# Three blocks on one Trainium2 core: decays of the state-space chunks from differences of prefix sums, and x weighed on GpSimd

## The chip, the core and the metric

The program runs on one core of one Trainium2 chip. The metric is the time of one execution on the device in microseconds (us), the median of the runs. Engines: TensorE (PE, its weight loads PEld), VectorE (DVE), ScalarE (ACT), GpSimd (POOL) and SyncE (SP), which here only asks for transfers.

## What is computed

Three blocks follow one another on x of 1024 tokens by 1024 features in fp32: stick-breaking attention with SwiGLU, a convolution and retention block, and a block with an S5 branch and a state-space branch (SSD) side by side. The change lies in the SSD branch alone. It has 16 heads of width 64, 4 groups, a state of 128:

```python
xd = (xs * dt[..., None])                       # x weighed by its step width
a = dt * A;  a_cs = jnp.cumsum(a, axis=-1)      # A < 0, one value per head
L_intra = jnp.exp(segsum(a))                    # exp(cs[l] - cs[s]) for s <= l, else 0
y_diag = einsum(einsum(Ch, Bh) * L_intra, xd)   # within a chunk
decay_states = jnp.exp(a_cs[..., -1:] - a_cs)   # x weighed by its decay to the chunk's end
states = einsum(Bh, decay_states, xd)           # carried on from chunk to chunk
y_off = einsum(Ch, prev_states, jnp.exp(a_cs))
y = gated_group_rmsnorm(y_diag + y_off + D * xs, z, norm_w)
```

## The kernel before

Everything is feature-major: 8 tiles of 128 features by 1024 tokens. Nearly all of TensorE's time goes into weight products in three parts (x high and low by w high and low, L650, L653, L654); GpSimd splits each weight panel into high and low parts (L609, L611, and L597 for panels that carry gains), SP loads the panels. Each engine has its own program, written out by hand in order, and waits on counters.

**The SSD stage** (ssd_out, about 3110 to 3248 us) takes 8 chunks of 128 tokens. All inputs are already in DRAM (spills). For chunk c, SP loads f (x, B and C of the chunk, 1 MB, double-buffered, L572) and zf (the gate z, L576). In the order of TensorE's queue:

- turn_x (L1221) transposes x; ScalarE copies it to xt (L1922); VectorE makes xd = xt * dt (L2769) and xe = xd * decay (L2781)
- turn_y (L1290) of the chunk before; scores (L1233) C by B; VectorE masks them into sm (L2786)
- decays (L1245): four products of the 0/1 matrix "after" with mt. mt holds, for each of 16 heads, the matrix "upto" times the step decays da (16 small ScalarE activations, L1781). The product is the sum of the decays between two tokens; ScalarE takes its Exp into lt (L1932); VectorE multiplies lt by sm (L2794)
- turn_b (L1228), direct (L1256, D * x), inter (L1272, C by the state), sums (L1299, the norm's sums of the chunk before, from ScalarE's Square L1945), intra (L1262, lt by xd), new (L1282, B by xe)

VectorE adds up y (L2802, L2808) and the state (L2813, L2818), makes the low part of the result before (low, L2842), the gate product gz (L2830) and the scaling (L2836). ScalarE's order for a step is: xt, Exp, bt (L1939), Square of the chunk before, half of mt for the chunk after next, the norm's Ln and Exp (L1950, L1953), the other half of mt, xh (L1957). Behind the Exp of chunk 0 ScalarE also asks for h back from DRAM (4 MB, L1964).

**Ahead of it**, the last tiles of xBC and of z run, and between their halves TensorE does the S5 outputs (s5_outputs, L775), whose results ScalarE's queue stores by 8 transfers each (y_store, L1824). At xBC tile 15 TensorE forms the prefix sums of da for all chunks (dec_sum, L1199) into bank 3. In the first z_last tile ScalarE makes mt of chunk 0. dec (L1914) is the Exp of the prefix sums, the tail sums and the totals; TensorE's first turn_x waits for it. On SP, the loads of f stand behind the last weight panels, and eight stores of the last S5 outputs (L581) behind zf of chunk 1.

Of the kernel before, what the change touches and what calls it, by code (L numbers as in the profile page):

```python
# [13 lines left out]
P = 128  # L14
# [249 lines left out]
def build(nc, ins, out, last=None):  # L264
# [5 lines left out]
    with ctx:  # L270
# [141 lines left out]
        with ExitStack() as st:  # L412
# [6 lines left out]
            mt = sb("mt", [P, SSD_HEADS, P], F32, st)  # L419
# [23 lines left out]
        y_spill = dram("y_spill", [D, S5_TAU, S5_BLOCKS])  # L443
        h_spill = dram("h_spill", [P, KT, T])
# [3 lines left out]
        seg_banks = [5, 0, 1, 5]  # L448
# [68 lines left out]
        def _(sp):  # L517
# [29 lines left out]
            else:  # L547
# [40 lines left out]
        def _(pool):  # L588
# [24 lines left out]

            def turn(name, i, before):
# [33 lines left out]
        def _(pe):  # L648
# [515 lines left out]
            if "s5_u" in run:  # L1164
# [37 lines left out]

                def within_xbc(e):
# [10 lines left out]
                for m in range(2):  # L1214
                    tile_x(units("z_last") + 2 * m, panels("z_last") + m, between=lambda: s5_outputs(6 + m))

            def ssd_turn_x(c):

                pe.wait_ge(S(f"f_in{c % 2}"), (c // 2 + 1) * 16)
                for q in range(8):  # L1220
# [16 lines left out]
            def ssd_decays(c):  # L1237

                pe.wait_ge(S("mt_ready"), c + 1)
                for q in range(4):  # L1240
                    if q == 1:
                        pe.wait_ge(S("xt_ready"), c + 1)
                    if q == 3:
                        pe.wait_ge(S("lt_ready"), 4 * c + 1)
                    nc.tensor.matmul(banks[seg_banks[q]][:, :], M["after"],  # L1245
                                     mt[:, 4 * q:4 * q + 4, :].rearrange("p h t -> p (h t)"),
                                     start=True, stop=True).then_inc(S("seg_done"), 1)

# [18 lines left out]
            def ssd_inter(c):  # L1267
                pe.wait_ge(S("state_ready"), c + 1)
                pe.wait_ge(S("sm_ready"), c + 1)
                pe.wait_ge(S("lt_ready"), 4 * c + 4)  # L1270
# [43 lines left out]
            if "ssd_out" in run:  # L1314
# [5 lines left out]
                ssd_decays(0)  # L1320
                ssd_turn_b(0)
                ssd_direct(0)
                for c in range(CHUNKS):
# [34 lines left out]
        def _(act):  # L1358
# [416 lines left out]
            def ssd_steps(c, part):  # L1775

                act.wait_ge(S("da_ready"), 1)
                if c:
                    act.wait_ge(S("seg_done"), 4 * c)
                for hd in range(8 * part, 8 * part + 8):  # L1780
                    mm = A(mt[:, hd, :], M["upto"], ACT.Copy, scale=da[:, c, hd:hd + 1])  # L1781
                if part:
                    mm.then_inc(S("mt_ready"), 1)

            if "s5_u" in run:
# [127 lines left out]
                act.wait_ge(S("dec_sum"), 1)  # L1913
# [11 lines left out]
            def ssd_exp(c):  # L1925
# [4 lines left out]
                for q in range(4):  # L1930
# [29 lines left out]
            if "ssd_out" in run:  # L1960
# [5 lines left out]
                for part in range(2):  # L1966
                    ssd_steps(1, part)
                for c in range(CHUNKS):
# [74 lines left out]
        def _(dve):  # L2043
# [711 lines left out]
            def heads(t, q):  # L2755
                return t[:, q * 512:(q + 1) * 512].rearrange("p (h d) -> p h d", d=SSD_P)

            def per_head(t, q):
                return t[:, 8 * q:8 * q + 8].unsqueeze(2).broadcast_to([P, 8, SSD_P])

            def ssd_weigh_x(c):

                dve.wait_ge(S("xt_ready"), c + 1)
                if c:
                    dve.wait_ge(S("intra_done"), c)
                else:
                    dve.wait_ge(S("spilled0"), 16 * 20)
                for q in range(2):
                    mm = V.tensor_tensor(heads(xd, q), heads(xt, q), per_head(dt[:, c, :], q), ALU.mult)  # L2769
                mm.then_inc(S("xd_ready"), 1)  # L2770

            def ssd_decay_x(c):

                dve.wait_ge(S("xd_ready"), c + 1)
                dve.wait_ge(S("dec_ready"), 1)
# [285 lines left out]
```

## Time and profile before

| what | us |
|---|---|
| median of 3 runs (lowest, highest) | 3666.65 (3662.11, 3667.56) |
| the profiled execution's own time | 3663.11 |
| its span | 3661.3 |
| PE busy | 3538.3 (97%) |
| DVE, POOL, ACT busy | 2080.5, 1093.3, 935.3 |

The span is what the profiler saw from the first to the last instruction; the time also holds what lies around it. Matmuls are pipelined: a matmul's duration is longer than the step to the next one, so the chain of waits, which counts from step to step, tells what a group of them costs.

### The profile page before, as it was taken

How to read it: one execution, taken by the hardware profiler on the slowest of the kernel's cores; microseconds unless marked ns; L12 is line 12 of the kernel's file. 1: busy time of each engine (PE TensorE's matmuls, PEld its weight loads, DVE VectorE, ACT ScalarE, POOL GpSimd, SP SyncE). 2: the span in 40 equal slices, each digit the busy share in tenths (PEclk: the TensorE clock that was granted, in tenths of full speed). 3: DMA queues.
4: the chain of work that ended last, by engine and by line, in shares of the span. 5: the costliest groups of instructions: out<-in, count | busy, mean ns of one | idle time of the engine just before them, and what ended most of it. 6: DMA issues, size and time to landing. Idle time of an engine off the chain costs nothing. (4 is left out here: it accounts for less than half of the span.)

```text
span 3661.3 us, 46083 instructions
## 1 busy us (share of the span) xinstructions
PE 3538.3 (97%) x18166; PEld 2876.8 (79%) x18166; DVE 2080.5 (57%) x2838; ACT 935.3 (26%) x1662; POOL 1093.3 (30%) x1069
## 2 busy tenths in 40 slices
PE   7999999999999999999999999799999999999998
PEld 5777776688888888788888888588878878787776
DVE  6464557524233236699945555644535697753564
ACT  4444445300000004311111100411221123652132
POOL 2221121233333333233332233033332234024332
PEclk9999999999999999999999999999999999999999
DMA  2010010212212111122221121221293224432211
GB/s 100 24 30 30 24 35 13 75 58 62 70 57 74 57 57 58 35 98 86 86 81 70 41 81 65 91 87 41 87 181 86 82 78 131 145 103 75 73 54 64
DMA packets 139240, 260.19 MB, mean 71 GB/s; under 512 B 45632, under 2 KB 87616, under 8 KB 136000
## 3 DMA queue, kind: packets, MB, share of 16 engines
q1 hardware_dynamic: 73360, 156.78, 14.7%
q10 hardware_dynamic: 65712, 101.10, 8.1%
q8 instruction: 114, 1.87, 0.2%
q14 instruction: 54, 0.44, 0.0%
HBM read 209.35 MB, written 46.14 MB: 70 GB/s over the span
## 5 line engine op out<-in xcount | busy, mean ns | idle before, releaser
L650 PE MATMUL bank<-xh,wh 128*128 128x512 f32 x3024 | 1192.8, 394 | 30.1 <-DVE xl L2107 12.1
L653 PE MATMUL bank<-xl,wh 128*128 128x512 f32 x3024 | 1183.1, 391 | 0.0
L654 PE MATMUL bank<-xh,wl 128*128 128x512 f32 x3024 | 1181.9, 391 | 0.0
L609 POOL CAST wh<-raw 128x512 fp32r<-128x512 f32 x528 | 345.7, 655 | 2364.4 <-PE bank L654 2202.5
L611 POOL TENSOR_TENSOR wl<-raw,wh 128x512 fp32r<-128x512 f32 x528 | 733.9, 1390 | 42.3
L650 PEld LDWEIGHTS bank<-xh,wh 128*128 128x128 f32 x3024 | 569.4, 188 | 168.0 <-issue 18.7
L654 PEld LDWEIGHTS bank<-xh,wl 128*128 128x128 f32 x3024 | 569.5, 188 | 122.3 <-issue 0.7
L653 PEld LDWEIGHTS bank<-xl,wh 128*128 128x128 f32 x3024 | 570.0, 188 | 118.0 <-issue 1.3
L2407 DVE SCALAR_TENSOR_TENSOR bank<-apad,cols,bank 128x512 f32<-128x512 f32 x406 | 267.9, 751 | 0.0
L2145 DVE TENSOR_TENSOR h<-bank,h 128x512 f32<-128x512 f32 x240 | 165.6, 691 | 145.5 <-PE bank L654 144.8
L2276 DVE TENSOR_TENSOR gt<-sa,bank 128x512 f32<-128x512 f32 x44 | 30.3, 688 | 347.8 <-PE bank L654 347.8
L2242 DVE TENSOR_TENSOR_SCAN fb<-fb,own_key 128x256 f32<-128x256 f32 (+7 forms) x128 | 174.3, 1403 | 68.4 <-ACT ab L1469 68.3
L650 PE MATMUL bank<-wh,xh 128*128 128x256 f32 x512 | 148.0, 289 | 0.4 <-POOL wl L611 0.4
L653 PE MATMUL bank<-wl,xh 128*128 128x256 f32 x512 | 144.8, 283 | 0.0
L654 PE MATMUL bank<-wh,xl 128*128 128x256 f32 x512 | 144.7, 283 | 0.0
L650 PE MATMUL bank<-gh,wh 128*128 128x512 f32 x352 | 138.2, 393 | 0.0
L654 PE MATMUL bank<-gh,wl 128*128 128x512 f32 x352 | 137.1, 390 | 0.0
L653 PE MATMUL bank<-gl,wh 128*128 128x512 f32 x352 | 136.9, 389 | 0.0
L2148 DVE SCALAR_TENSOR_TENSOR h<-bank,mod,h 128x512 f32<-128x512 f32 x128 | 95.3, 750 | 69.6 <-PE bank L654 69.0
L1521 ACT ACTIVATE sa<-bank 128x512 f32<-128x512 f32 x44 | 26.3, 599 | 390.1 <-DVE msum L2312 258.9
L2709 DVE SCALAR_TENSOR_TENSOR spill<-xc,cols,spill 128x1024 f32<-128x1024 f32 x48 | 69.0, 1438 | 96.5 <-ACT spill L1844 95.3
L1468 ACT ACTIVATE fb<-bank 128x512 f32<-128x512 f32 (+2 forms) x192 | 95.9, 500 | 87.7 <-PE bank L905 87.4
(339 smaller groups left out, 4876.9 us busy)
## 6 DMA issues: line engine op xcount, KB each, us to landing
raw<-in_wstream SPq DMA_DIRECT2D x264, 512.0 KB, 3.5
spills<-spill ACTq DMA_DIRECT2D x38, 512.0 KB, 2.9
rawm<-in_mod_w ACTq DMA_DIRECT2D x12, 1024.0 KB, 4.9
gate_spill<-gates ACTq DMA_DIRECT2D x16, 512.0 KB, 2.6
tabs<-in_rope ACTq DMA_DIRECT2D x4, 2048.0 KB, 8.9
f<-spills SPq DMA_DIRECT2D x8, 1024.0 KB, 5.6
h<-in_x ACTq DMA_DIRECT2D x4, 1024.0 KB, 11.8
tabs<-gate_spill ACTq DMA_DIRECT2D x4, 1024.0 KB, 7.4
```

Source lines behind the costliest of these rows:

```text
L609: nc.gpsimd.tensor_copy(wh[:, slot, k], raw[:, slot, k]).then_inc(S("panel_high"), 1)
L611: nc.gpsimd.tensor_tensor(wl[:, slot, k], raw[:, slot, k], wh[:, slot, k].bitcast(F32), ALU.subtract).then_inc(S("panel_split"), 1)
L650: mm = nc.tensor.matmul(o, lh, rh, start=start, stop=False, skip_group_check=shared)
L653: nc.tensor.matmul(o, lh, rl, start=False, stop=False, skip_group_check=shared)
L654: return nc.tensor.matmul(o, ll, rh, start=False, stop=stop, skip_group_check=shared)
L1468: A(fb[:, g % 2, a, s], banks[2 + n % 3][:, :w], ACT.Sigmoid, scale=-1.0)
L2145: V.tensor_tensor(h[:, n, t], banks[th][:, :], h[:, n, t], ALU.add).then_inc(S(f"bank_free{th}"), 1)
L2148: V.scalar_tensor_tensor(h[:, n, t], banks[th][:, :], gates(n), h[:, n, t], ALU.mult, ALU.add).then_inc(S(f"bank_free{th}"), 1)
L2242: V.tensor_tensor_scan(f_, f_, own_key[:, T - w:T][:, ::-1], 0.0, ALU.mult, ALU.max).then_inc(S("scanned"), 1)
L2276: V.tensor_tensor(gt[:, th, :], sa[:, th, :], banks[u.b % 2][:, :], ALU.mult).then_inc(S(f"bank_free{u.b % 2}"), 1)
L2407: V.scalar_tensor_tensor(o, a_in, w, o, ALU.mult, ALU.add).then_inc(S("conv_step"), 1)
L2709: V.scalar_tensor_tensor(o, a_in, w, o, ALU.mult, ALU.add).then_inc(S("x_step" if k < SSD_TAPS - 1 else "xo_ready"), 1)
```

## The change

The sum of decays between two tokens is the difference of two prefix sums. TensorE's decays products and ScalarE's mt go. Instead the prefix sums from dec_sum are copied with their sign turned into dtmp (one column per chunk and head), transposed by TensorE (cs_turn), copied again and stored to DRAM (cs_rows, 64 KB). SP loads for each chunk the rows of its 16 heads, the same 8 KB to all 128 partitions (csb, 1 MB). ScalarE forms |csb + dtmp| for each head (16 Abs), then four Exp with scale -1. The mask is applied in four parts, and intra waits for each. xd and xe are made by GpSimd.

```diff
-            mt = sb("mt", [P, SSD_HEADS, P], F32, st)
+            csb = sb("csb", [P, SSD_HEADS, P], F32, st)
...
+        cs_rows = dram("cs_rows", [P, P])
-        seg_banks = [5, 0, 1, 5]
+        cs_turned = msum[:, 0:P]
...
@@ SyncE, before the loads of f and zf of chunk c
                 for c in range(CHUNKS):
+                    if c:
+                        sp.wait_ge(S("lt_spans"), 4 * c)
+                    else:
+                        sp.wait_ge(S("cs_stored"), 16)
+                        sp.wait_ge(S("pc_ready"), KT)
+                    sp.dma_start(csb[:, :, :].rearrange("p h t -> p (h t)"),
+                                 cs_rows.rearrange("(c h) t -> c (h t)", c=CHUNKS)[c:c + 1].broadcast_to(
+                                     [P, SSD_HEADS * P])).then_inc(S("csb_in"), 16)
...
@@ GpSimd, behind the split of the first two ssd_out panels; both functions as VectorE had them, on pool
+                if name == "ssd_out" and i is None:
+                    for c in range(CHUNKS):
+                        ssd_weigh_x(c)
+                        ssd_decay_x(c)
...
@@ TensorE
+                def cs_turn():
+                    pe.wait_ge(S("cs_kept"), 1)
+                    nc.tensor.transpose(banks[2][:, 0:P], dtmp[:, :, :].rearrange("p c h -> p (c h)"), M["ident"]
+                                        ).then_inc(S("dec_sum"), 1)
...
-                    tile_x(units("z_last") + 2 * m, panels("z_last") + m, between=lambda: s5_outputs(6 + m))
+                    def within_z():
+                        if m == 0:
+                            cs_turn()
+                        s5_outputs(6 + m)
+
+                    tile_x(units("z_last") + 2 * m, panels("z_last") + m, between=within_z)
...
             def ssd_turn_x(c):
+                if c:
+                    pe.wait_ge(S("xt_ready"), c)
...
-            def ssd_decays(c):
...
             def ssd_intra(c):
-                pe.wait_ge(S("w_masked"), c + 1)
+                pe.wait_ge(S("xd_ready"), c + 1)
                 for hd in range(SSD_HEADS):
+                    if hd % 4 == 0:
+                        pe.wait_ge(S("w_masked"), 4 * c + hd // 4 + 1)
...
@@ ScalarE
-            def ssd_steps(c, part):
...
+                act.wait_ge(S("dec_sum"), 1)
+                A(dtmp[:, :, :].rearrange("p c h -> p (c h)"), banks[3][:, 0:P], ACT.Copy, scale=-1.0
+                  ).then_inc(S("cs_kept"), 1)
                 for m in range(2):
                     unit = units("z_last") + 2 * m
...
                     if m == 0:
-                        act.wait_ge(S("pc_ready"), KT)
-                        for part in range(2):
-                            ssd_steps(0, part)
                         y_store(6)
+                        act.wait_ge(S("dec_sum"), 2)
+                        A(cs_turned, banks[2][:, 0:P], ACT.Copy, scale=-1.0).then_inc(S("cs_kept"), 1)
+                        act.wait_ge(S("cs_kept"), 2)
+                        act.dma_start(cs_rows[:, :], cs_turned).then_inc(S("cs_stored"), 16)
...
@@ ScalarE, ssd_exp(c)
-                for q in range(4):
-                    act.wait_ge(S("seg_done"), 4 * c + q + 1)
-                    A(lt[:, 4 * q:4 * q + 4, :], banks[seg_banks[q]][:, :].rearrange("p (h t) -> p h t", t=P),
-                      ACT.Exp).then_inc(S("lt_ready"), 1)
+                act.wait_ge(S("csb_in"), 16 * c + 16)
+                for hd in range(SSD_HEADS):
+                    mm = A(lt[:, hd, :], csb[:, hd, :], ACT.Abs, bias=dtmp[:, c, hd:hd + 1])
+                    if hd % 4 == 3:
+                        mm.then_inc(S("lt_spans"), 1)
+                for g in range(SSD_GROUPS):
+                    act.wait_ge(S("lt_spans"), 4 * c + g + 1)
+                    A(lt[:, 4 * g:4 * g + 4, :], lt[:, 4 * g:4 * g + 4, :], ACT.Exp, scale=-1.0
+                      ).then_inc(S("lt_ready"), 1)
...
@@ VectorE, ssd_weights(c); its calls of ssd_weigh_x and ssd_decay_x go
-                V.tensor_tensor(l4, l4, sm[:, :, :].unsqueeze(2).broadcast_to([P, SSD_GROUPS, 4, P]), ALU.mult
-                                ).then_inc(S("w_masked"), 1)
+                for g in range(SSD_GROUPS):
+                    dve.wait_ge(S("lt_ready"), 4 * c + g + 1)
+                    l4 = lt[:, 4 * g:4 * g + 4, :]
+                    V.tensor_tensor(l4, l4, sm[:, g, :].unsqueeze(1).broadcast_to([P, 4, P]), ALU.mult
+                                    ).then_inc(S("w_masked"), 1)
```

What this does to the order of instructions, at three places.

ScalarE ahead of the stage: the copy of the prefix sums (dtmp) between the eight stores of y_store(5) and the first half of z's first tile (xd). Before:

```order
L1824 DMA y_spill<-u 16x8x128 [waits s5_added]
L1824 DMA y_spill<-u 16x8x128 x7
L1899 ACTIVATE xd<-bank 128x512 [waits unit_done]
L1830 ACTIVATE spill<-spill 128x1024 [waits xo_ready]
L1832 DMA spills<-spill 128x1024 [waits xs_ready]
L1899 ACTIVATE xd<-bank 128x512 [waits unit_done]
L1906 DMA spills<-xd 128x1024 [waits spilled0,bank_free1,bank_free0]
L1781 ACTIVATE mt<-mats,da 128x128 [waits da_ready,pc_ready]
L1781 ACTIVATE mt<-mats,da 128x128 x7
```

Now, with msum the transposed sums:

```order
L1856 DMA y_spill<-u 16x8x128 [waits s5_added]
L1856 DMA y_spill<-u 16x8x128 x7
L1928 ACTIVATE dtmp<-bank 128x128 [waits dec_sum]
L1934 ACTIVATE xd<-bank 128x512 [waits unit_done]
L1862 ACTIVATE spill<-spill 128x1024 [waits xo_ready]
L1864 DMA spills<-spill 128x1024 [waits xs_ready]
L1934 ACTIVATE xd<-bank 128x512 [waits unit_done]
L1941 DMA spills<-xd 128x1024 [waits spilled0,bank_free1,bank_free0]
L1856 DMA y_spill<-u 16x8x128 [waits s5_added]
L1856 DMA y_spill<-u 16x8x128 x7
L1945 ACTIVATE msum<-bank 128x128 [waits dec_sum]
L1947 DMA cs_rows<-msum 128x128 [waits cs_kept]
```

The copy into dtmp is new in front of the xd eviction, and the 16 mt activations are replaced by one copy and a store behind y_store(6).

ScalarE in one step of the loop (from taking x of chunk c+1 to xh of chunk c). Before:

```order
L1922 ACTIVATE xt<-bank 128x512 [waits xd_ready,x_turned]
L1922 ACTIVATE xt<-bank 128x512
L1932 ACTIVATE lt<-bank 128x512 [waits seg_done,intra_done]
L1932 ACTIVATE lt<-bank 128x512 [waits seg_done] x3
L1939 ACTIVATE bt<-bank 128x512 [waits new_done,b_turned]
L1945 ACTIVATE sq<-gz 128x1024 [waits ssd_sum,gz_ready]
L1781 ACTIVATE mt<-mats,da 128x128 [waits seg_done,da_ready]
L1781 ACTIVATE mt<-mats,da 128x128 x7
L1950 ACTIVATE bank<-bank,eps 128x512 [waits ssd_sum]
L1953 ACTIVATE bank<-bank 128x512 [waits rs_log]
L1781 ACTIVATE mt<-mats,da 128x128 [waits seg_done,da_ready]
L1781 ACTIVATE mt<-mats,da 128x128 x7
```

Now:

```order
L1957 ACTIVATE xt<-bank 128x512 [waits xd_ready,x_turned]
L1957 ACTIVATE xt<-bank 128x512
L1967 ACTIVATE lt<-csb,dtmp 128x128 [waits csb_in,intra_done]
L1967 ACTIVATE lt<-csb,dtmp 128x128 x15
L1972 ACTIVATE lt<-lt 128x512 [waits lt_spans] x4
L1979 ACTIVATE bt<-bank 128x512 [waits new_done,b_turned]
L1985 ACTIVATE sq<-gz 128x1024 [waits ssd_sum,gz_ready]
L1990 ACTIVATE bank<-bank,eps 128x512 [waits ssd_sum]
L1993 ACTIVATE bank<-bank 128x512 [waits rs_log]
L1997 ACTIVATE xh<-gz 128x8x128 [waits gn_ready]
```

The 16 small activations, before in two halves behind the Square (sq), are now ahead of Exp, bt and the Square.

SP at the first two chunks, before (u is the S5 output) and now:

```order
L572 DMA f<-spills 128x16x128 [waits spilled1,spilled0]
L576 DMA zf<-spills 128x8x128 [waits spilled1,spilled0]
L572 DMA f<-spills 128x16x128
L576 DMA zf<-spills 128x8x128
L581 DMA y_spill<-u 16x8x128 [waits s5_added]
```

```order
L580 DMA csb<-cs_rows 128x2048 [waits pc_ready,cs_stored]
L588 DMA f<-spills 128x16x128 [waits spilled1,spilled0]
L592 DMA zf<-spills 128x8x128 [waits spilled1,spilled0]
L580 DMA csb<-cs_rows 128x2048 [waits lt_spans]
L588 DMA f<-spills 128x16x128
L592 DMA zf<-spills 128x8x128
L597 DMA y_spill<-u 16x8x128 [waits s5_added]
```

A load of csb is new in front of each load of f, and the second one waits for lt_spans, the Abs of chunk 0.

## Rows read from the trace of the kernel before

**Rows 1.** The page, part 1: busy time, share of the span, instructions

```profile
PE 3538.3 (97%) x18166; PEld 2876.8 (79%) x18166; DVE 2080.5 (57%) x2838; ACT 935.3 (26%) x1662; POOL 1093.3 (30%) x1069
```

**Rows 2.** Chain of waits, one chunk (3179 to 3197) and one start: start us, us, line

```profile
3128.04 0.87 PE bank L1221 x8
...
3179.17 0.87 PE bank L1221 x8
...
3181.81 3.44 PE bank L1245 x8
...
3185.68 1.79 PE bank L1256 x16
3187.47 1.73 PE bank L1272 x8
3189.20 1.72 PE bank L1299 x4
3190.91 3.52 PE bank L1262 x32
...
3196.22 0.87 PE bank L1221 x8
```

**Rows 3.** Timeline of ScalarE: start us, us, line, operation, count [idle before]

```profile
3118.32 4.78 ACT L1781 ACTIVATE mt<-mats,da 128x128 f32<-128x128 f32 x16
...
3180.08 1.08 ACT L1922 ACTIVATE xt<-bank 128x512 f32<-128x512 f32 x2 [1.60 <-PE bank L1221]
...
3186.26 1.06 ACT L1945 ACTIVATE sq<-gz 128x1024 f32<-128x1024 f32 x1
```

**Rows 4.** Timeline of VectorE, the same chunk

```profile
3181.40 1.22 DVE L2842 TENSOR_TENSOR xl<-gz,xh 128x1024 fp32r<-128x1024 f32 x1
3182.54 1.29 DVE L2769 TENSOR_TENSOR xd<-xt,dt 128x512 f32<-128x512 f32 x2
3183.74 1.28 DVE L2830 TENSOR_TENSOR gz<-zf,bank 128x512 f32<-128x512 f32 x2
```

**Rows 5.** Timeline of TensorE, entry to the stage

```profile
3086.29 2.15 PE L775 MATMUL bank<-h,pb 64*128 64x127 f32 x32
...
3110.43 1.94 PE L1221 MATMUL bank<-mats,f 128*128 128x128 f32 x8 [3.14 <-ACT dec L1914]
```

**Rows 6.** Timeline of ScalarE, the same entry

```profile
3084.26 5.80 ACTq L1824 DMA_DIRECT2D y_spill<-u  x8
...
3094.82 0.36 ACTq L1906 DMA_DIRECT2D spills<-xd  x1
```

**Rows 7.** TensorE, timeline, then a stretch: us, PE busy, PEclk, DMA share, GB/s

```profile
2337.23 0.47 PE L650 MATMUL bank<-rh,wh 128*128 128x512 f32 x1 [1.97 <-DVE h L2148]
...
2338.70:2342.10 3.40, 2.82 (x8) 0.50 0.45 154
```

**Rows 8.** DMA, 3060 to 3262: issuer, count, KB, us to landing; SP's timeline

```profile
f<-spills SPq DMA_DIRECT2D x8, 1024.0 KB, 5.6
...
h<-h_spill ACTq DMA_DIRECT2D x1, 4096.0 KB, 14.4
...
y_spill<-u ACTq DMA_DIRECT2D x30, 64.0 KB, 2.9
...
y_spill<-u SPq DMA_DIRECT2D x8, 64.0 KB, 11.8
...
3094.67 0.39 SPq L572 DMA_DIRECT2D f<-spills  x1
```

**Rows 9.** DMA queues, 3117 to 3132: packets, MB, share of 16 engines

```profile
q10 hardware_dynamic: 144, 4.19, 71.2%
q1 hardware_dynamic: 2117, 1.01, 23.0%
```

**Rows 10.** Lines L597 (GpSimd) and L2709 (VectorE): ns min/median/max

```profile
L597 POOL TENSOR_TENSOR raw<-raw,cols x8: 1890/1898/2882, 3083.2 to 3308.0; 128x1024 f32<-128x1024 f32 x8
...
L2709 DVE SCALAR_TENSOR_TENSOR spill<-xc,cols,spill x48: 1270/1285/2806, 2665.6 to 3087.2; 128x1024 f32<-128x1024 f32 x48
```

More of the change, by code:

```diff
@@ L446, in build, with heads, per_head @@
         block = ctx.enter_context(nc.Block())
-        seg_banks = [5, 0, 1, 5]
+        cs_turned = msum[:, 0:P]
+        def heads(t, q):
+            return t[:, q * 512:(q + 1) * 512].rearrange("p (h d) -> p h d", d=SSD_P)
+        def per_head(t, q):
+            return t[:, 8 * q:8 * q + 8].unsqueeze(2).broadcast_to([P, 8, SSD_P])
         def settled(eng):
@@ L612, in split, with ssd_weigh_x, ssd_decay_x @@
                                             ALU.subtract).then_inc(S("panel_split"), 1)
+            def ssd_weigh_x(c):
+                pool.wait_ge(S("xt_ready"), c + 1)
+                if c:
+                    pool.wait_ge(S("intra_done"), c)
+                else:
+                    pool.wait_ge(S("spilled0"), 16 * 20)
+                for q in range(2):
+                    mm = nc.gpsimd.tensor_tensor(heads(xd, q), heads(xt, q), per_head(dt[:, c, :], q), ALU.mult)
+                mm.then_inc(S("xd_ready"), 1)
+            def ssd_decay_x(c):
+                pool.wait_ge(S("xd_ready"), c + 1)
+                pool.wait_ge(S("dec_ready"), 1)
+                if c:
+                    pool.wait_ge(S("new_done"), c)
+                else:
+                    pool.wait_ge(S("spilled1"), 16 * 20)
+                for q in range(2):
+                    mm = nc.gpsimd.tensor_tensor(heads(xe, q), heads(xd, q), per_head(dec[:, 1, c, :], q), ALU.mult)
+                mm.then_inc(S("xe_ready"), 1)
             def turn(name, i, before):
@@ L1214, in _ @@
                 for m in range(2):
-                    tile_x(units("z_last") + 2 * m, panels("z_last") + m, between=lambda: s5_outputs(6 + m))
+                    def within_z():
[3 more added lines that the diff above has]
+                    tile_x(units("z_last") + 2 * m, panels("z_last") + m, between=within_z)
             def ssd_turn_x(c):
                 pe.wait_ge(S(f"f_in{c % 2}"), (c // 2 + 1) * 16)
+                if c:
+                    pe.wait_ge(S("xt_ready"), c)
                 for q in range(8):
@@ L1235, in ssd_scores @@
                 mm.then_inc(S("bc_done"), 1)
-            def ssd_decays(c):
-                pe.wait_ge(S("mt_ready"), c + 1)
-                for q in range(4):
[L1241 to L1247, printed above, removed]
             def ssd_direct(c):
@@ L1773, in spill_tiles @@
                         act.dma_start(spills[n * 2 + (first + m)], spill[:, m, :]).then_inc(S(f"spilled{m}"), 16)
-            def ssd_steps(c, part):
[L1777 to L1783, printed above, removed]
             if "s5_u" in run:
@@ L1929, in ssd_exp @@
                     act.wait_ge(S("intra_done"), c)
-                for q in range(4):
-                    act.wait_ge(S("seg_done"), 4 * c + q + 1)
-                    A(lt[:, 4 * q:4 * q + 4, :], banks[seg_banks[q]][:, :].rearrange("p (h t) -> p h t", t=P),
-                      ACT.Exp).then_inc(S("lt_ready"), 1)
+                act.wait_ge(S("csb_in"), 16 * c + 16)
[7 more added lines that the diff above has]
+                      ).then_inc(S("lt_ready"), 1)
             def ssd_take_b(c):
@@ L1965, in _ @@
                 ssd_take_b(0)
-                for part in range(2):
-                    ssd_steps(1, part)
                 for c in range(CHUNKS):
@@ L2753, in _ @@
                 s5_add(7)
[L2755 to L2775, printed above, removed]
-                if c:
-                    dve.wait_ge(S("new_done"), c)
-                else:
-                    dve.wait_ge(S("spilled1"), 16 * 20)
-                for q in range(2):
-                    mm = V.tensor_tensor(heads(xe, q), heads(xd, q), per_head(dec[:, 1, c, :], q), ALU.mult)
-                mm.then_inc(S("xe_ready"), 1)
             def ssd_mask(c):
@@ L2844, in _ @@
             if "ssd_out" in run:
-                ssd_weigh_x(0)
-                ssd_decay_x(0)
                 ssd_mask(0)
@@ L2865, in _ @@
                         ssd_weights(c + 1)
-                        ssd_decay_x(c + 1)
                     ssd_scale(c)
```

12 lines of the change are left out of this document (removed).

## The prediction

> **What bounds the kernel now.** I read the page's busy shares first, then the chain of waits in the stage that changes, then what ScalarE and VectorE do there, then the entry to the stage and its transfers. TensorE is busy for 97% of the span [rows 1], so what matters is TensorE's queue. The chain shows what it does in one chunk of the state-space stage [rows 2]: from one turn of x (L1221) to the next it is 3196.22 - 3179.17 = 17.05 us, all of it TensorE, without a gap. Of this the decay sums (L1245) take 3.44 us. ScalarE and VectorE are hidden under it. So taking L1245 out promises 8 x 3.44 = 27.5 us, and the question is what stands right behind TensorE, and what the replacement costs at the entry. A measurement of this kernel can tell about 0.2%, 7.3 us, from no change.
>
> **The steady chunk.** TensorE's own work falls to 17.05 - 3.44 = 13.61 us. Before, the 16 small activations of a chunk (mt) ran two chunks ahead, in ScalarE's idle time. Their successors, 16 Abs of the same 128x128 form, stand in ssd_exp: behind take_x of the same chunk, and ahead of take_b and of the previous chunk's Square. That closes a loop, because TensorE's order is inter(c+1), sums(c), intra(c+1), and sums(c) waits for that Square. With its pieces, counted from the end of intra(c): new (L1282, from 3190.91 + 3.52 = 3194.43 to 3196.22, 1.78 in the chain) and turn_x 0.87 [rows 2] make 2.65. Taking x is two evictions, 0.98 before the next may start (1.08 for both, the second's end overlapping) [rows 3]. For the 16 Abs no row exists. The nearest is the mt group: 16 in 4.78, one every 0.29, so 4.69 of occupancy [rows 3]; the bounds are 3.2 (if a read of plain data with a bias took 0.2 each) and 6.3 (each at its full 0.39, if nothing overlapped). I take 4.69, the same shape. Then 4 Exp at the eviction's 0.49, 1.96; one eviction for b, 0.49; Square 1.06 [rows 3]. Then sums 1.72 and intra 3.52 [rows 2]. The sum is 2.65 + 0.98 + 4.69 + 1.96 + 0.49 + 1.06 + 1.72 + 3.52 = 17.07, and with some 0.2 for handing over between engines 17.3 us. So **the loop through ScalarE is as long as the TensorE work that it replaces**: 7 chunks x (17.3 - 17.05) = **+1.8 us**. With the bounds of Abs it is 15.8 to 18.9 a chunk, -9 to +13.
>
> What lies beside it: xd and xe move to GpSimd, 4 operations of 128x512 a chunk. The nearest GpSimd row multiplies by a broadcast column, 128x1024 in 1.90 [rows 10], so about 1.0 each and 4 us; up to 5.8 if it is disturbed as in that group's longest, 2.88. They begin when x is taken (3.6) and are done by 7.6 to 9.4, while intra wants xd at 13.6 and new wants xe at 17. They cost nothing; cover gone, the bill starts only above 6 us more. VectorE loses 2.6 us of work in a chunk. Splitting the mask into four lets it follow each Exp. VectorE still has to give the gate. In the chunk before, intra (L1262) ended at 3194.43 - 17.05 = 3177.4 and gz at 3183.74 + 1.28 = 3185.0, 7.6 later, with 1.2 of xd ahead of it that goes away [rows 2, 4]: gz at 6.4, then direct (1.79) and inter (1.73) to 9.9 [rows 2], against the Square's end at 11.8. That is 1.9 us of slack. GpSimd's work falls on this very piece. In the one place where a three-operation VectorE group meets a GpSimd multiply, one VectorE operation of 1.28 became 2.81 and GpSimd's 1.90 became 2.88 [rows 10]: both slowed down, together about by the shorter one's length. One such meeting (low with xd) is about 1 us and fits in the slack. The Trainium skill (SBUF — State Buffer, its table of terms) says that the pair of ports is locked for a whole instruction and the loser blocks fully; by it low could wait for both xd operations, and the sum would be up to 3 us longer over 7 chunks.
>
> **Entry, the new wait.** cs_turn stands on TensorE between the two halves of the first z_last tile, where it waits for ScalarE's copy of the prefix sums (cs_kept). In ScalarE's queue this copy is behind the 8 store issues of y_store(5), which last until 3084.26 + 5.80 = 3090.06 [rows 6]. TensorE is there at 3086.29 [rows 5]. The copy takes 0.39 like mt, so TensorE stands from 3086.3 to about 3090.6: 4.3 us, and queued behind it are s5_outputs(6) and the half tile; z's evictions, y_store(6), the last outputs and dec wait for those. After a wait of 3.14 us before 3110.43, eight transposes took 1.94 [rows 5] where the chain has 0.87 for the same eight [rows 2]; behind a shorter wait elsewhere the granted clock was 0.50, 1.2 GHz, through a stretch of 3.4 us [rows 7]. Such a stretch does half of its work; the same after this wait costs some 1.7. With the transpose **+6.1 us**.
>
> **Entry, the transfers.** Before, f of chunk 0 was asked for at 3094.67 and lay ready long before turn_x(0) at 3110.43 [rows 5, 8]. Now SP first waits for cs_stored. z's store goes out at 3094.82 + 6.1 = 3100.9 [rows 6]; y_store(6) takes 5.8 as y_store(5) did; the copy and its issue 0.8; a 64 KB store 2.9 to land [rows 8]. So csb(0) is asked for at about 3110.4. f takes 5.6 alone; csb is as large (1024 KB) and in the same queue ahead of it. h, four times as large, lands in 14.4, so 1 MB more is some (14.4 - 5.6) / 3 = 2.9, say 3.0 [rows 8]: f(0) lands 5.6 + 3.0 = 8.6 after, at 3119.0, a little later with z's spill between. turn_x(0) starts at 3119.7 where it could have at 3110.43 + 6.1 = 3116.5: **+3.2 us**. Bounds: 0 (csb lands for nothing) and 6 (128 reads of one 8 KB row at half the rate).
>
> **Chunk 0.** Before, 3128.04 - 3110.43 = 17.61 from turn_x(0) to turn_x(1) [rows 2, 5]. Now, with the first transposes at the low clock as before: 1.94 + 0.98 + 4.69 + 1.96, the last quarter of the mask 0.7 (low is 1.22 for twice the columns), the last quarter of intra 0.9, new 1.78 = 12.95, since nothing of a chunk before stands in between. **-4.7 us.** VectorE's dd is ready earlier, too, without xd and xe.
>
> **f of chunk 1.** This is the largest term. f(1) was issued at once behind f(0); now it is behind csb(1), and that waits for the Abs of chunk 0 (lt_spans), 1.94 + 0.98 + 4.69 = 7.6 after turn_x(0) begins. At the same moment ScalarE, past its Exp, asks for h (4096 KB, 14.4 to land) [rows 8]. What such a neighbour does can be seen: eight 64 KB stores of SP that lie beside h took 11.8 to land, ScalarE's own of that size 2.9 [rows 8]; and while h moved, its queue passed 144 packets with 4.19 MB and SP's queue 1.01 MB in 2117 small ones, most of them before h began or after it ended [rows 9]. So packets take turns, not bytes. csb(1) has 8 KB packets against h's 32 KB ones, and f(1), of 512 B packets behind csb, gets little until both are done. h landed 14.4 after its issue with 0.5 MB of stores beside it; csb is 0.5 MB more, 1.6; then f's 3.0. f(1) lands 7.6 + 19.0 = 26.6 after turn_x(0), while TensorE is ready at 12.95. **+13.7 us**, and 0.9 for a cold clock after it. Bounds: csb and f alone need 8.6, so f at 16.2, +3.3; all of csb behind all of h, +15. I take the value near the upper bound, since the stores beside h behaved so. In later chunks f is asked for at 8.8 of the loop and wanted at 17.3 + 1.8 = 19.1, over 10 us later; 8.6 fits.
>
> **Clock in between.** The new loop leaves TensorE idle for 17.3 - 13.6 = 3.7 us a chunk in two pieces, 1.6 before direct (from turn_b's end at 4.8) and 1.9 before sums. After a wait of 1.97 at 2337 the clock was at 0.50 for the next stretch [rows 7]. Part of this lies under slack; **+1.5 us** in all, between 0 and 12.
>
> **The sum:** 6.1 + 3.2 - 4.7 + 13.7 + 0.9 + 1.8 + 1.5 = +22.5, on the profiled execution's 3663.11, which is 3.5 under the median of the runs shown. On the median 3666.65 it is 3689.
>
> **Rivals.**
> (1) f(1) is less late, since the queues share by bytes, or csb slips in ahead of h. Then the 13.7 falls to between 3 and 7: 3678 to 3682. Against it are the 11.8 us stores.
> (2) The clock falls in every chunk. Each fall is a stretch of 3.4 us at half speed, 1.7 lost: 7 x 1.7 = 12, less the 1.5 counted: 3699.5. For it: the 1.97 row; against it: most of a gap here is shorter. The Trainium skill (TensorE: Matmul & The Clock Gate, HAM oscillation) describes exactly this, a loop with a wait in each round that starts cold each time; the trace shows single cases of it only.
> (3) GpSimd blocks VectorE for all its 4 us: gz at 10.4, direct and inter to 13.9, past the Square by 2.1, 7 x 2.1 = 15: 3704. For it: both operands of low lie in SBUF like those of the disturbed row; against it: gate and mask read a bank, and VectorE's operations of that kind showed no such stretching.
> (4) The other side: faster. If the ScalarE steps between turn_x and sums(c) come to 3 us less than my 9.2 (Abs at 0.2 each and Exp from SBUF cheaper), the loop is 14.3, nearly TensorE's 13.6, and 7 chunks give -19; with the entry (+9.3 - 4.7) and f(1) hidden by half (+6) 3658. It decides below a loop of 14.5 us. Against it is the row of 16 in 4.78.
> (5) No change: the entry wait is small and f(1) nearly in time: -4.7 + 1.8 and some 4, 3668.
>
> **How the numbers follow.** My forecast 0.47 (its own range 3683 to 3695), rival 1 0.19, rival 2 0.12, rival 3 0.10, rival 4 0.05, rival 5 0.07. Slower by over 0.2% (above 3674): 0.47 + 0.19 + 0.12 + 0.10 = 0.88; within: 0.07; faster: 0.05. The range 3674 to 3702 leaves out rivals 4 and 5 and half of 3.
>
> **What would show it.** Right: a TensorE wait of about 4 us for a transpose of dtmp at 3086; turn_x(0) waiting for f, not dec; a wait of over 10 us for f before turn_x(1), with csb and f landing late beside h; a period of 17.3 with Square waiting for nothing and sums waiting for Square; no wait for xd or xe. Wrong: a period near 13.6 to 15 us, f(1) landing within 9 us of csb's issue, or direct waiting for gz longer than sums for Square.

## The result, and the profile after

| what | before | after |
|---|---|---|
| median of 5 runs (lowest, highest) | 3665.72 (3662.11, 3667.56) | **3685.29** (3683.16, 3688.55) |
| span of the profiled execution | 3661.3 | 3683.5 |
| PE, DVE, POOL, ACT busy | 3538.3, 2080.5, 1093.3, 935.3 | 3520.8, 2068.5, 1133.1, 933.6 |

The kernel is slower by 0.55%: the ratio is 1.0055, with a 95% interval of 1.0044 to 1.0066, so 19.6 us at the medians. TensorE works 17.5 us less than in [rows 1] and the time grows, so in the profiled executions, whose spans differ by 22.2, it stands idle for some 40 us more. The waits of TensorE say where.

TensorE's waits in the changed kernel from 3060 to 3300 us (line, what it waited for: us in all, times, longest):

```profile
PE bank L1299 <- DVE gz L2836: 15.6, 6, 2.6
PE bank L1276 <- DMA f<-spills: 10.6, 1, 10.6
PE bank L1343 <- ACT sq L1985: 5.1, 5, 1.7
PE bank L1248 <- ACT dtmp L1928: 3.5, 1, 3.5
PE bank L1276 <- ACT dec L1949: 3.1, 1, 3.1
PE bank L1299 <- DVE dd L2854: 2.5, 1, 2.5
```

Here L1276 is turn_x, L1299 direct, L1343 sums, L1248 the transpose cs_turn. Only the wait for dec was there at this size before [rows 5].

TensorE's timeline at the entry, in chunks 0 and 1 (start us, us, line, operation, count, idle before it):

```profile
3093.40 0.34 PE L1248 MATMUL bank<-mats,dtmp 128*128 128x128 f32 x1 [3.50 <-ACT dtmp L1928]
3093.66 3.71 PE L818 MATMUL bank<-h,pb 64*128 64x127 f32 x32
...
3119.37 1.06 PE L1276 MATMUL bank<-mats,f 128*128 128x128 f32 x8 [3.14 <-ACT dec L1949]
...
3124.26 3.68 PE L1299 MATMUL bank<-dd,f 128*128 128x128 f32 x16 [2.50 <-DVE dd L2854]
...
3133.03 1.95 PE L1326 MATMUL bank<-xe,bt 128*128 128x256 f32 x8
3145.57 1.97 PE L1276 MATMUL bank<-mats,f 128*128 128x128 f32 x8 [10.60 <-DMA f<-spills]
```

**Entry.** cs_turn waits for the copy into dtmp, and the 32 small products behind it (L818) take 3.71 where they took 2.15 [rows 5]: a wait, then the low clock. turn_x of chunk 0 starts 8.9 us later than before [rows 5]. Not all of it is the change's: TensorE came to this place at 3089.9 where it had come at 3086.3 [rows 5], and the program up to there is the same on it. The 3.6 us are there at 2720 already: TensorE's waits for the low parts of weights from GpSimd add up to 12.6 there and to 9.0 in the kernel before. It is taken as scatter between executions: in the experiments, none of which changes TensorE's work up to there, it came between 3083.9 (e5) and 3093.2 (e8). The rest, 8.94 - 3.6 = 5.3, belongs to the change: the wait of 3.50, the transpose 0.26, and 3.71 - 2.15 = 1.56 for the low clock. turn_x of chunk 0 waits for dec, not for f.

**The second f.** DMA issues between 3126 and 3131 us (what, issuer, count, KB, us to landing):

```profile
h<-h_spill ACTq DMA_DIRECT2D x1, 4096.0 KB, 16.5
csb<-cs_rows SPq DMA_DIRECT2D x1, 1024.0 KB, 16.4
f<-spills SPq DMA_DIRECT2D x1, 1024.0 KB, 18.9
```

csb, h and f are asked for within half a microsecond; csb and h land together, and f, which stands behind csb, 2.9 us later. csb comes in 128 pieces of 8 KB and h in 128 of 32 KB, and the pieces of both run through the whole of this time side by side. Over all 8 chunks csb takes a median of 4.8, beside h 16.4. That is f's 10.6 us wait.

**The loop.** ScalarE and VectorE in one steady chunk, then GpSimd:

```profile
3182.70 1.09 ACT L1957 ACTIVATE xt<-bank 128x512 f32<-128x512 f32 x2 [2.55 <-PE bank L1276]
3183.68 4.78 ACT L1967 ACTIVATE lt<-csb,dtmp 128x128 f32<-128x128 f32 x16
3188.35 2.18 ACT L1972 ACTIVATE lt<-lt 128x512 f32<-128x512 f32 x4
3190.43 0.58 ACT L1979 ACTIVATE bt<-bank 128x512 f32<-128x512 f32 x1
3190.91 1.05 ACT L1985 ACTIVATE sq<-gz 128x1024 f32<-128x1024 f32 x1
```

```profile
3184.02 1.97 DVE L2848 TENSOR_TENSOR xl<-gz,xh 128x1024 fp32r<-128x1024 f32 x1
3186.12 1.29 DVE L2836 TENSOR_TENSOR gz<-zf,bank 128x512 f32<-128x512 f32 x2
```

```profile
3183.87 3.02 POOL L638 TENSOR_TENSOR xd<-xt,dt 128x512 f32<-128x512 f32 x2 [12.42 <-ACT xt L1957]
```

ScalarE goes from xt to Square without a gap, as foretold. low (L2848) takes 1.97 instead of 1.22 [rows 4], because xd on GpSimd lies beside it, and gz follows it. Of xd's two operations the first takes 1.04, as it does alone, and the second, beside low, 2.02. The chain shows the period (start us, us, line):

```profile
3164.23 0.89 PE bank L1276 x8
...
3181.79 0.89 PE bank L1276 x8
```

3181.79 - 3164.23 = 17.56, against 17.05 before [rows 2]. From turn_x of chunk 1 to turn_y of chunk 7 it is 3145.57 to 3270.71, 125.1 us against 119.3 before: in three places there the clock falls as well, as it does at the entry and in direct of chunk 0. Three of these five stretches (from:to us, length, busy time of the engines, PEclk, DMA share, GB/s):

```profile
3093.30:3096.60 3.30, 3.20 (x27) 3.08 (x29) 0.00 (x0) 1.48 (x3) 0.00 (x0) 0.54 0.44 143
3137.70:3151.20 13.50, 5.63 (x27) 5.63 (x28) 1.50 (x3) 3.63 (x12) 2.38 (x3) 0.51 0.76 222
3206.00:3209.20 3.20, 3.20 (x14) 2.89 (x13) 2.50 (x4) 3.20 (x7) 0.58 (x1) 0.54 0.71 220
```

The granted clock near 0.5 is the 1.2 GHz level. The second stretch begins inside the wait for f and holds on through the first products after it; the third follows the wait for gz.

### The profile page after: what moved, and what is told of

Same layout as the page of the kernel before. It is cut to its first block and busy times, and to the rows that moved or that the text cites. A ratio compares the mean times of both kernels' runs of the same rounds, so it can differ in the third digit from the quotient of the medians.

```text
span 3683.5 us, 45993 instructions
## 1 busy us (share of the span) xinstructions
PE 3520.8 (96%) x18103; PEld 2871.0 (78%) x18103; DVE 2068.5 (56%) x2830; ACT 933.6 (25%) x1664; POOL 1133.1 (31%) x1101
## 5 line engine op out<-in xcount | busy, mean ns | idle before, releaser
L693 PEld LDWEIGHTS bank<-xh,wh 128*128 128x128 f32 x3024 | 568.5, 188 | 172.7 <-issue 22.2
```

Source lines behind the costliest of these rows:

```text
L693: mm = nc.tensor.matmul(o, lh, rh, start=start, stop=False, skip_group_check=shared)
```

## The experiments

The theory has four parts: the copy's place in ScalarE's queue costs some 5 us, h beside csb and f some 10, the Square behind Abs and Exp the loop, and GpSimd's half little. The main rival was that low's slowing by GpSimd rules the loop. Each kernel was timed against the kernel before on the same chip; ratios are to that one, with 95% intervals. An interval reaches 4 to 6 us to either side, about what a single edit is worth, so for single edits the waits in the trace carry the verdict and the time supports it. A second measure leaves out what happens ahead of the stage: in the profiled execution, the time from where TensorE is ready for the transpose of dtmp (in the kernel before, for the S5 products behind it) to turn_y of chunk 7. It is 160.9 in the kernel before and 180.7 in the changed one (one execution of each).

### e1_copy_early: the copy into dtmp earlier in ScalarE's queue

```diff
 first_tap(e)
+if e == 15:
+    act.wait_ge(S("dec_sum"), 1)
+    A(dtmp..., banks[3][:, 0:P], ACT.Copy, scale=-1.0).then_inc(S("cs_kept"), 1)
...
-act.wait_ge(S("dec_sum"), 1)
-A(dtmp..., banks[3][:, 0:P], ACT.Copy, scale=-1.0).then_inc(S("cs_kept"), 1)
```

> The changed kernel with one edit: ScalarE copies the prefix sums into dtmp before Silu of xBC tile 14 and the eight stores of y_store(5), instead of behind them. If the 3.50 us that TensorE stood before the transpose of dtmp comes from those stores alone: no wait there (under 0.3), the S5 products behind it back from 3.71 to 2.15 us, so turn_x(0) about 5 us earlier and the time about 5 us shorter, 3680 against 3685. Rival (the wait is absorbed later by the load of f for chunk 0, which the transfers then delay): turn_x(0) waits for f instead of dec and the time moves by under 2 us.

3680.38, ratio 1.0045 (1.0028 to 1.0063). TensorE's timeline:

```profile
3085.68 0.27 PE L1248 MATMUL bank<-mats,dtmp 128*128 128x128 f32 x1
3085.88 2.15 PE L818 MATMUL bank<-h,pb 64*128 64x127 f32 x32
...
3110.03 1.94 PE L1276 MATMUL bank<-mats,f 128*128 128x128 f32 x8 [3.14 <-ACT dec L1950]
```

The wait is gone, the 32 products are back at 2.15, and turn_x of chunk 0 is where it was before. So the wait and its cold clock were the entry's 5.3 us. From the transpose to turn_y(7) it is 176.6, 4.0 less than in the change: turn_x(0) runs at the low clock again, 1.94 instead of 1.06.

### e2_h_late: h is fetched behind the last step of chunk 1

```diff
 ssd_take_x(0)
 ssd_exp(0)
-act.wait_ge(S("s5_carried"), KT)
-act.dma_start(h[:, :, :], h_spill[:, :, :])
 ssd_take_b(0)
 ...
     ssd_high(c)
+    if c == 1:
+        act.wait_ge(S("s5_carried"), KT)
+        act.dma_start(h[:, :, :], h_spill[:, :, :])
```

> The changed kernel with one edit: ScalarE asks for h (4 MB) behind chunk 1's last step instead of behind the Exp of chunk 0. If f(1) is late because csb(1) takes turns with h packet by packet: csb(1) lands in about 5 us instead of 16.4, f(1) in 7.5 instead of 18.9, TensorE's wait for f before turn_x(1) falls from 10.6 to under 1.5 us, and the time is 9 to 12 us shorter, unless h then delays the load of a later chunk by as much: h beside csb(2) or csb(3) would show the same wait of 8 to 11 us at that chunk. Rival (csb itself, 128 reads of the same 8 KB, is slow and h does not matter): the wait stays above 8 us and csb(1) stays above 12.

3677.68, ratio 1.0037 (1.0025 to 1.0048). Issues in the same place, without h:

```profile
csb<-cs_rows SPq DMA_DIRECT2D x1, 1024.0 KB, 4.7
f<-spills SPq DMA_DIRECT2D x1, 1024.0 KB, 7.5
```

TensorE waits for no f. From turn_x(0) to turn_x(1) it is 17.05 instead of 26.2, that is 9.1 less. The time falls by 7.6, where 9 to 12 was expected; to turn_y(7) the trace has 173.3, 7.3 less. Some of it is given back in the next chunk:

```profile
3144.46 3.42 PE L1343 MATMUL bank<-sq,mats 128*128 128x512 f32 x4 [3.15 <-ACT sq L1985]
```

With f early, TensorE is ahead of ScalarE, stands 3.15 for the Square and runs the sums at the low clock. Further on, h lies beside the transfers of a later chunk, where they have time: no wait.

### e10_f_first: SP asks for f ahead of csb

```diff
 for c in range(CHUNKS):
+    ...
+    sp.dma_start(f[:, c % 2], spills[3 * KT:3 * KT + 16, :, t]...)
     if c:
         sp.wait_ge(S("lt_spans"), 4 * c)
     ...
     sp.dma_start(csb..., cs_rows...)
-    ...
-    sp.dma_start(f[:, c % 2], spills[3 * KT:3 * KT + 16, :, t]...)
```

> The changed kernel with one edit on SP: in each chunk f is asked for ahead of csb. f(1) is then on its way before h. Theory (csb takes turns with h packet by packet, whatever stands behind it): TensorE's wait for f before turn_x(1) is gone, but csb(1), asked for at the same moment as before, still lands 15 to 16.5 us later, and now ScalarE's Abs of chunk 1 wait for it. The wait moves and shrinks, since xt and the rest of chunk 0 are done by then: about 6 us gained of the 10.6, 3679 to 3681 against 3685. Rival (f was late for its own small packets, csb does not matter): Abs of chunk 1 do not wait, 10 us or more gained, 3675 or less.

3682.80, ratio 1.0047 (1.0033 to 1.0062), only 2.5 less than the change where 4 to 6 was expected, and too little to tell from none by the time alone. f(1) lands in 6.2 and TensorE doesn't wait for it, but csb now takes up to 17.7. ScalarE's waits, then TensorE's timeline:

```profile
ACT lt L1967 <- DMA csb<-cs_rows: 6.6, 1, 6.6
```

```profile
3154.64 3.43 PE L1343 MATMUL bank<-sq,mats 128*128 128x512 f32 x4 [9.86 <-ACT sq L1985]
```

ScalarE waits 6.6 for csb in front of its Abs of chunk 1, and TensorE 9.86 for the Square behind them. The wait moved from one engine's operand to another's, and the sums behind it run at the low clock. From turn_x(0) to turn_x(2) it is 42.5 instead of 44.7. It is h beside the two, far more than their order, that costs.

### e3_square_first: Square ahead of the four Exp

```diff
     mm.then_inc(S("lt_spans"), 1)
+if c:
+    ssd_square(c - 1)
 for g in range(SSD_GROUPS):
```

> The changed kernel with one edit: Square of the chunk before stands between the Abs and the Exp of ssd_exp, instead of behind Exp and the eviction of b. Theory (the loop of 17.56 us runs through ScalarE up to Square and sums): Square ends 2.4 us earlier, sums follows inter without a wait, and the loop falls to what VectorE then allows: from sums through the norm's root, VectorE's eight operations up to gz (9.6), direct, inter and sums (5.2), 16.3 us; 6 loops give 7 to 8 us less, 3677 to 3679. Rival (the loop was bound by gz, late because of GpSimd): 17.5 us still, no change. Rival (TensorE's own 13.6 us is what is left): 14 us a loop, 20 us less.

3674.60, ratio 1.0035 (1.0025 to 1.0046). TensorE's timeline:

```profile
3193.63 1.04 PE L1276 MATMUL bank<-mats,f 128*128 128x128 f32 x8
...
3199.47 2.05 PE L1299 MATMUL bank<-dd,f 128*128 128x128 f32 x16 [2.59 <-DVE gz L2839]
...
3210.10 1.04 PE L1276 MATMUL bank<-mats,f 128*128 128x128 f32 x8
```

The period falls from 17.56 to 16.47 (16.3 was expected), and no wait for the Square is left. From turn_x(1) to turn_y(7) it is 117.4 instead of 125.0, the 7 to 8 us of the theory; the medians differ by more, 10.7. So the Square's place did set the loop. But it does not fall to TensorE's 13.6: a second loop stands right behind. The chain of this kernel gives its pieces, from sums to sums: sums 1.73, ScalarE's Ln and Exp of the norm 0.67 and 0.59, VectorE's scale 1.16, ys 2.60, state 2.54, low 1.90, gz 1.34, direct 2.05, inter 1.73, with the gaps 16.47 (3186.78 to 3203.25). It goes through VectorE.

### e4_weigh_vectore and e7_vectore_square_first: xd and xe back on VectorE

The same edit once in the changed kernel (e4) and once in e3 (e7):

```diff
 # GpSimd
-for c in range(CHUNKS):
-    ssd_weigh_x(c)
-    ssd_decay_x(c)
 # VectorE
     if c:
         ssd_low(c - 1)
+    if c + 1 < CHUNKS:
+        ssd_weigh_x(c + 1)
     ssd_gate(c)
     ...
         ssd_weights(c + 1)
+        ssd_decay_x(c + 1)
```

> The changed kernel with xd and xe back on VectorE, at their old places. Theory (ScalarE's loop is the bound, VectorE has slack): low falls from 1.97 to 1.2 us, xd takes 1.2 in its place, gz comes at the same moment or 0.3 us later, the loop stays at 17.6, and in chunk 0 the later dd vanishes in the wait for f(1): the time is the same within 2 us. Rival (GpSimd's work held up VectorE and so the loop): 1 us less a loop, 7 us less in all. Rival (the move to GpSimd is worth the 2.6 us a chunk that VectorE loses): 10 us or more longer.

> e3 (Square between Abs and Exp) with xd and xe on VectorE. In e3 VectorE's chain up to gz bounds the loop, at 16.46. If that is so, work put back on it now shows: xd 1.2 us more ahead of gz, low 0.75 less without GpSimd beside it, so 16.9 to 17.4 a loop, 3 to 6 us more than e3's 3674.6. Rival (xd and xe never matter): 16.46 still and the same time within 1.5 us.

e4: 3687.68, ratio 1.0062 (1.0045 to 1.0080), which can't be told from the change's 1.0055. The period stays 17.56, set by the Square. e7: 3683.39, ratio 1.0044 (1.0030 to 1.0057), 8.8 above e3 where 3 to 6 was expected. TensorE's waits in e4 and in e7:

```profile
PE bank L1272 <- DVE gz L2832: 17.7, 6, 3.6
PE bank L1272 <- DVE dd L2852: 4.3, 1, 4.3
```

```profile
PE bank L1272 <- DVE gz L2835: 17.4, 7, 2.8
PE bank L1272 <- DVE dd L2855: 4.8, 1, 4.8
```

The GpSimd half of the change is worth little while the Square sets the loop, and 9 us at the medians once it doesn't. Little of that is VectorE's own work: e7's period in chunks at the full clock is 16.70, below the 16.9 expected and 0.23 above e3's, 1.6 us in 7 chunks. Behind the chunk that follows the wait for f, four chunks in e7 have a stretch at the low clock and take 1.4 to 3.0 us more, in e3 two. low takes 1.22 in e4, so GpSimd does slow VectorE in the change, but xd's own 1.2 on VectorE outweighs the 0.75 saved, and direct waits for gz 2.82 instead of 2.60. GpSimd isn't what costs.

### e8_before_pool_x: the kernel before, with that half of the change alone

The edit of e4 the other way round, in the kernel before.

> The kernel before with one half of the change alone: xd and xe on GpSimd, the decays still on TensorE. Theory (TensorE's 17.05 us bound the loop before and VectorE had nearly 3 us of slack): the loop stays at 17.05 and the time the same within 2 us; chunk 0 may gain up to 1.2 us, since dd is ready earlier. Rival (GpSimd slows VectorE through the memory they share, so that gz is late for direct): a wait for gz before direct in every chunk, 0.5 us or more a loop.

3664.03, ratio 0.9996 (0.9987 to 1.0005): the same. TensorE's timeline:

```profile
3150.24 1.04 PE L1255 MATMUL bank<-mats,f 128*128 128x128 f32 x8
...
3167.29 1.04 PE L1255 MATMUL bank<-mats,f 128*128 128x128 f32 x8
```

The period is 17.05, TensorE's own, as in [rows 2]. Chunk 0 is shorter (by the timeline 3133.20 - 3117.31 = 15.89 instead of 3127.87 - 3110.43 = 17.44), since dd comes sooner and the wait of 1.20 for it is gone. The GpSimd half costs nothing by itself; the loss comes in with the decays.

### e5_three_edits and e6_pool_state_low: does it add up, and is there a better kernel?

e5 has the diffs of e1, e2 and e3 together. e6 adds to e5 (VectorE's multiplication of the state goes too; it isn't shown):

```diff
 # GpSimd, per chunk
     ssd_weigh_x(c)
     ssd_decay_x(c)
+    ssd_fade(c)          # state * decay of the chunk, as VectorE had it
+    if c:
+        ssd_low(c - 1)   # gz - high part, as VectorE had it
 # VectorE
-    if c:
-        ssd_low(c - 1)
```

> The changed kernel with the three edits together: the copy into dtmp early, h asked for behind chunk 1, Square between Abs and Exp. If the three are separate terms they add: 4.9 + 7.6 + 10.7 = 23 us under 3685, some 3662, the same as before within 0.2%. No wait for dtmp, none above 1.5 us for f, a loop of 16.4 us. If they overlap (the loop's edit had only used the time of the others), 3668 or more.

> e5 with two more pieces of VectorE's chain on GpSimd: the multiplication of the state by its decay and, for chunks 0 to 6, the low part. If VectorE's chain up to gz bounds the loop in e3 and e5 (16.4), then without its 1.3 and 1.97 us gz comes 3 us earlier; ScalarE's Abs up to the Square is next, at 14.7 to 15 us a loop: 6 to 7 loops give 9 to 11 us under e5, 3651 to 3654, faster than the kernel before. Rival (GpSimd is then too slow: low and the state at about 2 to 3 us each behind xd and xe, with the gate waiting for low): 16.4 or more, no gain.

e5: 3662.93, ratio 0.9994 (0.9985 to 1.0003). The single edits gave 4.9, 7.6 and 10.7, in sum 23.2; together they give 22.4. Counted by the distances to the kernel before as it was timed beside each, it is 2.6, 5.3 and 8.4, in sum 16.3, against 21.8, so the sizes of the single ones are known to some 3 us. By the trace, from the transpose to turn_y(7), e3 has 174.8 and e5 159.4, so the three give 4.0, 7.3 and 5.9, in sum 17.2, and together 21.3. Each wait goes with its own edit; that the times simply add up is not shown. Without these costs the change is worth nothing: the same as before. e6: **3655.71, ratio 0.9971 (0.9960 to 0.9982)**, 0.3% faster than the kernel before. Its TensorE timeline, then GpSimd's:

```profile
3142.33 1.04 PE L1292 MATMUL bank<-mats,f 128*128 128x128 f32 x8
...
3150.25 1.96 PE L1359 MATMUL bank<-sq,mats 128*128 128x512 f32 x4 [0.85 <-ACT sq L2004]
...
3157.59 1.04 PE L1292 MATMUL bank<-mats,f 128*128 128x128 f32 x8
```

```profile
3144.56 2.04 POOL L638 TENSOR_TENSOR xd<-xt,dt 128x512 f32<-128x512 f32 x2 [1.22 <-ACT xt L1974]
...
3149.48 2.04 POOL L657 TENSOR_TENSOR state<-state,dec 128x512 f32<-128x512 f32 x2 [0.75 <-PE bank L1332]
```

The period is 15.26, 1.8 below before's and somewhat above the 14.7 to 15 expected. The wait for gz is gone, which shows that the second loop was VectorE's. The rest is a wait of 0.85 for the Square behind 16 Abs, and xd is back at 2.04 since low no longer lies beside it.

### e9_square_in_abs: Square between the 8th and the 9th Abs, f first, in e6

The edit of e10 is in it too and isn't shown again:

```diff
 for hd in range(SSD_HEADS):
+    if c and hd == SSD_HEADS // 2:
+        ssd_square(c - 1)
     mm = A(lt[:, hd, :], csb[:, hd, :], ACT.Abs, bias=dtmp[:, c, hd:hd + 1])
 ...
-if c:
-    ssd_square(c - 1)
```

> e6 (loop 15.26, bound by ScalarE up to Square) with Square between the eighth and the ninth Abs, and f asked for ahead of csb. Theory: Square is then done before inter ends, so TensorE's own work of 13.6 us is the bound, 13.7 to 14.1 a loop, without a wait for Square or gz above 0.3: 6 loops give 7 to 9 us under e6's 3655.7, and the waits for f (1.7) go: 3645 to 3649. Rival (the masks, which follow the Exp, now hold up intra because Exp is later): a wait of intra for lt, 14.6 or more a loop, 3651 to 3654.

3658.21, ratio 0.9983 (0.9975 to 0.9992): not better than e6. One of TensorE's waits, a piece of the chain (start us, us), then a stretch and the same stretch of the next chunk but one:

```profile
PE bank L1323 <- DVE lt L2821: 7.7, 7, 1.1
```

```profile
3170.12 1.36 DVE lt L2821
```

```profile
3154.40:3161.20 6.80, 6.80 (x29) 6.23 (x29) 3.97 (x6) 1.29 (x2) 2.35 (x1) 0.54 0.96 325
3188.50:3195.30 6.80, 6.80 (x29) 5.97 (x28) 3.70 (x6) 1.06 (x1) 2.35 (x1) 0.54 0.27 80
```

The wait for the Square is gone, and intra waits 1.1 for the first quarter of the mask in its place, as in the rival. The Exp did not move: from the first xt to the first Exp it is 6.60 us in e6 and in e9, since 16 Abs and the Square lie between them in either order. A second path, as long as the first, goes through Exp, the mask and intra, so chunks at the full clock still take 15.3 (3161.69 to 3176.99). The first quarter of the mask takes 1.36, where the other three take 0.68: GpSimd's multiplication of the state, which e6 put there, runs until 3170.92 beside it. By these two numbers the wait would be 0.4 without it (an estimate that no run checks). Three times the clock falls right behind the wait and the chunk takes 18.0 to 18.5. In e6's profiled execution no stretch at the same times is below 1.00.

## Why the prediction was right, and where its terms were off

**The direction and the main mechanism held.** 3685.3 was measured and 3689 forecast. Taking 3.44 us of products a chunk off TensorE gave no gain, because the loop through ScalarE is as long. What makes the kernel slower was foreseen in kind: the entry's wait, f of chunk 1 and the loop. That the total comes so near is in part luck: three terms were too high by 0.8, 3.2 and 3.1, and two too low by 2.7 and 1.6. The terms by one execution of each kernel, with the 3.6 us ahead of the stage left out:

| term | predicted | measured |
|---|---|---|
| entry, the wait for the copy and its clock | +6.1 | +5.3 |
| entry, transfers | +3.2 | 0 |
| chunk 0 | -4.7 | -2.0 |
| f of chunk 1 | +13.7 | +10.6 |
| loop, cold clock, clock in between | +4.2 | +5.8 |
| sum | +22.5 | +19.7 |

The measured sum agrees with the 19.6 between the medians. (The spans differ by 22.2: with the 3.6 ahead of the stage, and 1.2 less behind it.)

- **Entry, the new wait.** Right; e1 removes it. The wait was 3.50, not 4.3: the copy took 0.28 and the eight issues 4.93, not 5.80.
- **Entry, the transfers.** Wrong: turn_x(0) waited for dec and for no f. The mis-sized pieces are y_store(6), taken as 5.8 like y_store(5) and measured at 4.14, and the 64 KB store of cs_rows, 1.6 to land instead of 2.9. csb(0) was asked for at 3110.27, 9.1 us ahead of turn_x(0), and f(0), asked for at 3110.70, took 7.3 and had landed 1.4 us before turn_x(0).
- **Chunk 0.** Mis-sized, by the wrong path: the prediction followed ScalarE and said only in passing that dd would be ready earlier. TensorE came to direct so much sooner that it waited 2.50 for dd (1.20 before), and ran direct at the low clock, 3.68 instead of 2.05. Intra then began behind inter and not behind the last mask. From turn_x(0) to where turn_x(1) could start it was 3145.57 - 10.60 - 3119.37 = 15.60, not 12.95, though the first transposes ran at the full clock, 1.06 instead of the 1.94 assumed.
- **f of chunk 1.** Right in kind and time: f landed 26.2 after turn_x(0), forecast 26.6. The wait was smaller because chunk 0 was longer by 2.7. Rival 1 (the queues share by bytes) is refuted: csb, a quarter of h, took 16.4 beside it and landed with it, and 4.7 without it in e2.
- **The loop.** Predicted 17.3, measured 17.56, with 16 Abs in 4.78 as taken from mt. Half of the excess is the four Exp, 2.08 in the chain and not 1.96. Sums waited 0.85 instead of 1.9, and direct 2.60 instead of 1.6: the two idle pieces were forecast without the meeting of low and xd, which the prediction itself had put at 1 us. It cost 0.75, and what it adds to the wait for gz it takes from the one for the Square. (Its rows gave 2.81 - 1.28 = 1.53 and 2.88 - 1.90 = 0.98, in sum 2.5 and not the shorter operation's 1.28.) The total idle time, 3.5, is near the 3.7 forecast. That the Square is the bound e3 shows; the slack of gz was put at 1.9 us, of which the meeting left 0.9, and e3 shows 1.09 (17.56 - 16.47).
- **The clock.** The falls came in single chunks, as taken. From turn_x(1) on they cost 5.8 - 7 x 0.51 = 2.2, with 2.4 forecast; what was too low in that row of the table is the loop, 3.6 instead of 1.8. Two of them cost only some 0.6 each, since the wait for the Square, 0.85 in the other chunks, was gone there. Rival 2 (a fall in every chunk) did not happen in the changed kernel; of the kernels above e7 comes nearest, in five of the seven chunks from turn_x(1) on. The Trainium skill (TensorE: Matmul & The Clock Gate, HAM oscillation) describes a loop whose wait in each round cools the clock. The traces agree for single rounds; no kernel here does it in every round.
- **Rival 3** (GpSimd blocks VectorE for all its work) is refuted: low was held up by 0.75 and not by 4, and e4 took GpSimd away without a gain. The Trainium skill (SBUF — State Buffer, table of terms) has the loser block fully, for one whole instruction. The trace agrees, operation by operation: xd's first took 1.04 as alone, low, begun 0.15 after it, 0.75 more than alone, and xd's second, beside low, 2.02, ending 0.9 after low. So low waited for the rest of one operation, not for both, and the 3 us by this rule did not come.

What stays open: why e7's clock falls more often than e3's, which is most of its 8.8 us; whether the 3.6 us ahead of the stage are scatter alone; and whether the number of pieces is what decides how long csb takes beside h, since no run changed their size.

## What to carry to other kernels

Work taken off the busiest engine is worth only what the next loop leaves: add up the loop through the other engines, in queue order, before counting the gain, and look for the one behind it too (here 13.6, then 15.3, then 16.5, then 17.6). A small operation that others wait for, such as a Square or a copy, belongs ahead of bulk work in its queue, as long as no second path through the bulk work is as long (e9). A new load is priced by what moves at the same moment, not by its own time.

## What was not expected of the hardware

- **A short wait can be followed by the low clock.** In e9 waits of 1.1 us stood ahead of stretches of 6.8 us at the 1.2 GHz level, three times; in e6 waits of 0.85 in each chunk had none, and waits of 2.6 in the changed kernel had it in some chunks only. What decides between them these runs don't tell.
- **A queue with small packets was held back by one with large ones.** csb, 128 pieces of 8 KB, took 16.4 us beside h's 128 pieces of 32 KB, which took 16.5, and 4.7 to 4.8 in most other chunks: about one piece of one for one piece of the other.
- **VectorE and GpSimd held each other up by single operations.** low took 1.97 instead of 1.22 and xd's second operation 2.02 instead of 1.04 where they met; in e9 the first quarter of the mask took 1.36 instead of 0.68.
- **Reading the same 8 KB into all 128 partitions costs like an ordinary load:** 1 MB in 4.7 to 4.8 us; the prediction's upper bound had half the rate.
